# A PEER feed-forward block: 32 tokens taken out of the dense up products and computed from gathered expert rows

## The reference

```python
# T = 512 tokens, D = 1024, 8 heads, 128 x 128 = 16384 experts, top 16 per head
q = (ht @ peer_wq).reshape(T, 8, 2, 128)
s = einsum('thpd,hpkd->thpk', q, peer_keys)
sv, si = top_k(s, 16)                       # per half of the key
cand = sv[..., 0, :, None] + sv[..., 1, None, :]
top, pos = top_k(cand, 16)                  # 16 experts per token and head
eidx = ...                                  # expert = i * 128 + j
g = softmax(top)
u = peer_u[ib]                              # 128 expert rows per token
a = gelu(einsum('td,thkd->thk', hb, u))
out = einsum('thk,thkd->td', g * a, peer_v[ib])
```

## Time and profile before

| | |
|---|---|
| median of 3 runs | 1610.52 us |
| the profiled execution | 1606.33 us, span 1604.5 us |
| PE, weight loads, DVE, ACT, POOL busy | 99%, 86%, 83%, 40%, 25% of the span |
| granted TensorE clock | 1.00 |
| chain that ended last | PE 94%, DVE 3%, ACT 1% |
| HBM | 260 GB/s over the span, 413 in the fullest slice |

### The profile page before, as it was taken

How to read it: one execution, slowest core, us unless ns; L and a number is a source line. 1 busy time by engine, 2 the same in 40 slices (tenths; PEclk the granted TensorE clock), 3 DMA queues, 4 the chain that set the end, 5 groups by cost and what they waited for, 6 DMA issues and landing times.

```text
span 1604.5 us, 24652 instructions
## 1 busy us (share of the span) xinstructions
PE 1582.9 (99%) x8490; PEld 1382.4 (86%) x8490; DVE 1338.7 (83%) x2533; ACT 634.6 (40%) x978; POOL 406.6 (25%) x343
## 2 busy tenths in 40 slices
PE   8999999999999999999999999999999999999998
PEld 4777678887889999999998888888888888888887
DVE  6899787774899999999678888888888888888876
ACT  5433834235334445554333333333333333333332
POOL 0000001102435200001244334433343333433420
PEclk9999999999999999999999999999999999999999
DMA  9431245753324467868999999999999999999981
GB/s 339 144 106 40 99 165 185 254 185 120 109 82 151 156 208 251 279 227 259 387 413 387 352 345 332 333 360 358 343 331 328 357 356 349 329 326 359 355 312 69
DMA packets 168012, 418.79 MB, mean 261 GB/s; under 512 B 12673, under 2 KB 78337, under 8 KB 167810
## 3 DMA queue, kind: packets, MB, share of 16 engines
q1 hardware_dynamic: 115472, 247.92, 42.4%
q0 software_dynamic: 42960, 156.79, 27.3%
q10 hardware_dynamic: 9506, 13.12, 2.2%
HBM read 375.83 MB, written 41.95 MB: 260 GB/s over the span
## 4 chain that ended last, share of the span: by engine, by line
PE 94%; DVE 3%; ACT 1%; issue 1%; DMA 0%; DVEq 0%; ACTq 0%
PE bank L1575 18%; PE bank L1577 17%; PE bank L1576 17%; PE bank L1921 11%; PE bank L1922 11%; PE bank L1920 11%; PE bank L1899 3%; PE bank L1831 1%; DVE sb_scr L1086 1%; PE bank L1748 1%; PE bank L1607 1%; PE bank L1738 1%; PE bank L1609 1%; PE bank L1608 1%; DVE sb_scr L987 1%
## 5 line engine op out<-in xcount | busy, mean ns | idle before, releaser
L625 ACT ACTIVATE sb_w_hi<-sb_stage 128x1024 fp32r<-128x1024 f32 x324 | 343.2, 1061 | 541.8 <-PE bank L1922 323.7
L973 DVE TENSOR_TENSOR sb_w_lo<-sb_stage,sb_w_hi 128x1024 fp32r<-128x1024 f32 x294 | 359.4, 1224 | 169.8 <-ACT sb_w_hi L625 168.6
L1575 PE MATMUL bank<-sb_act_hi,sb_w_hi 128*128 128x384 f32 (+1 forms) x1408 | 498.1, 354 | 2.9 <-DVE sb_w_lo L973 2.2
L1577 PE MATMUL bank<-sb_act_hi,sb_w_lo 128*128 128x384 f32 (+1 forms) x1408 | 492.7, 350 | 0.0
L1576 PE MATMUL bank<-sb_act_lo,sb_w_hi 128*128 128x384 f32 (+1 forms) x1408 | 492.2, 350 | 0.0
L1922 PE MATMUL bank<-sb_w_hi,sb_mix_lo 128*128 128x512 f32 x768 | 300.1, 391 | 0.0
L1921 PE MATMUL bank<-sb_w_lo,sb_mix_hi 128*128 128x512 f32 x768 | 299.9, 391 | 0.0
L1920 PE MATMUL bank<-sb_w_hi,sb_mix_hi 128*128 128x512 f32 x768 | 298.8, 389 | 0.0
L1575 PEld LDWEIGHTS bank<-sb_act_hi,sb_w_hi 128*128 128x128 f32 x1408 | 264.4, 188 | 23.3 <-issue 4.4
L1576 PEld LDWEIGHTS bank<-sb_act_lo,sb_w_hi 128*128 128x128 f32 x1408 | 264.5, 188 | 17.3 <-issue 0.5
L1577 PEld LDWEIGHTS bank<-sb_act_hi,sb_w_lo 128*128 128x128 f32 x1408 | 264.2, 188 | 15.2
(11 more groups left out here) (244 smaller groups left out, 1814.6 us busy)
## 6 DMA issues: line engine op xcount, KB each, us to landing
sb_stage<-u_dram SPq DMA_DIRECT2D x128, 512.0 KB, 5.5
sb_stage<-v_dram SPq DMA_DIRECT2D x128, 512.0 KB, 6.0
sb_stage<-w_front_dram SPq DMA_DIRECT2D x68, 512.0 KB, 4.4
g_scratch<-sb_scr SPq DMA_DIRECT2D x12, 2048.0 KB, 8.8
sb_scr<-g_scratch SPq DMA_DIRECT2D x32, 768.0 KB, 8.0
sb_scr<-w_ada_dram POOLq DMA_DIRECT2D x32, 512.0 KB, 4.6
a_scratch<-sb_scr ACTq DMA_DIRECT2D x64, 192.0 KB, 4.0
sb_scr<-a_scratch SPq DMA_DIRECT2D x16, 768.0 KB, 11.7
```

Source lines behind the costliest of these rows:

```text
L625: nc.scalar.activation(w_hi[:, slot, :], stage[:, slot, :], ACT.Copy).then_inc(w_round, 1)
L973: nc.vector.tensor_tensor(w_lo[:, slot, :], stage[:, slot, :], w_hi[:, slot, :].bitcast(F32), ALU.subtract).then_inc(w_split, 1)
L1575: nc.tensor.matmul(out, w_hi[:, slot, w], rhs_hi[:, dc, :], start=(i == 0), stop=False)
L1577: last = nc.tensor.matmul(out, w_lo[:, slot, w], rhs_hi[:, dc, :], start=False, stop=(i == len(dcs) - 1))
```

## The change

The first 32 tokens of tile 0 (`NS`) leave the dense up products. These run over 352 columns (`NU`), and gelu too; the first 32 columns of `ga` are 1.0 all the time. The gates of these tokens are not made by one-hot products: part 0 of `g_scratch` is filled with zeros early, and for each pick the value weight x gelu(dot) is added into its place by an indirect DMA with addition. As the activation there is 1.0, gate times activation is then what it was.

The dots come from gathered rows. The 32 tokens have 128 picks each. They are laid out as 4 groups of 32 partitions, each group with the same 32 tokens and 32 of the picks, so 32 gathers of 128 rows do (`SPICKS`). For that PE copies the tokens' activations four times into rows (`sh2_ok`), DVE copies them from PSUM to `s_h`, and POOL copies the lists of expert numbers, places and weights to the four groups. DVE makes a dot per gather, two in most units from 1 to 18 of the gate stage, ACT two gelus, DVE two weight products, POOL 32 scatter-adds. The batches of the gate stage are 44 instead of 48: turn 0 has one in each unit. The diff below, cut to its core, shows the constants and tables first, then the parts of POOL, ACT, DVE and PE.

```diff
+NS = 32
+NU = ND - NS
+GROUPS = P // NS
+SPICKS = PICKS // GROUPS
+S_ROWS = 6
+S_HALF = SPICKS // 2
+S_FIRST = (1, 10)
+S_UNITS = 9
...
-def share(n, b):
-
-    return range(n * b // G_UNITS, n * (b + 1) // G_UNITS)
+def batches(it, b):
+
+    skip = S_BATCHES if it == 0 else 0
+    n = TURN_BATCHES - skip
+    return range(skip + n * b // G_UNITS, skip + n * (b + 1) // G_UNITS)
...
+def sparse_dots(u):
+
+    half = int(u >= S_FIRST[1])
+    k = u - S_FIRST[half]
+    return [S_HALF * half + d for d in range(S_HALF) if 0 <= k == d * S_UNITS // S_HALF]
...
             pool.wait_ge(m_ok, DC)
             pool.dma_start(keys[:, :, :], keys_d).then_inc(keys_in, 16)
+            nc.gpsimd.memset(zeros, 0.0).then_inc(gz_ok, 1)
+            pool.wait_ge(gz_ok, 1)
+            for k in range(4):
+                pool.dma_start(g_d[8 * k:8 * k + 8, :, 0:1, :].rearrange("a p n m -> p a (n m)"),
+                               zeros.rearrange("p (o m) -> p o m", o=1).to_broadcast([P, 8, P])).then_inc(gz_in, 16)
...
             pool.wait_ge(x2_out, 16)
...
+            def sparse_gather(d):
+                k = s_pick(d)
+                if d >= S_ROWS:
+                    pool.wait_ge(s_used, d - S_ROWS + 1)
+                pool.indirect_dma_start(s_row[d % S_ROWS], None, u_rows_d,
+                                        bass.IndirectOffsetOnAxis(ap=s_list.bitcast(U32)[:, 0, k:k + 1], axis=0)
+                                        ).then_inc(sg_in[d % S_ROWS], 16)
+
+            def sparse_add(d):
+
+                h, r = divmod(d, SPICKS // PH)
+                k = s_pick(d)
+                if r == 0 and h:
+                    pool.wait_ge(s_out, 16 * (SPICKS // PH) * h)
+                pool.indirect_dma_start(g_flat, bass.IndirectOffsetOnAxis(ap=s_list.bitcast(U32)[:, 1, k:k + 1], axis=0),
+                                        s_w[:, d:d + 1], None, compute_op=ALU.add).then_inc(s_out, 16)
+
+            pool.wait_ge(st_ok, 1)
+            for g in range(GROUPS):
+                pool.dma_start(s_list[g * NS:(g + 1) * NS, :, :],
+                               m_list[0:NS, :, g * SPICKS:(g + 1) * SPICKS]).then_inc(sl_in, 16)
+            pool.wait_ge(sl_in, 16 * GROUPS)
+            pool.wait_ge(gz_in, 64)
+            for d in range(S_HALF + S_ROWS):
+                sparse_gather(d)
+            pool.wait_ge(sw_ok, 1)
+            for d in range(S_HALF):
+                sparse_add(d)
+                if S_HALF + S_ROWS + d < SPICKS:
+                    sparse_gather(S_HALF + S_ROWS + d)
+            pool.wait_ge(sw_ok, 2)
+            for d in range(S_HALF, SPICKS):
+                sparse_add(d)
             pool.wait_ge(idx_ok, 1)
...
-                    nc.scalar.activation(ga[:, k % 2, :], UB[k][:, 0:ND], ACT.Gelu).then_inc(ge_ok, 1)
+                    nc.scalar.activation(ga[:, k % 2, NS:ND], UB[k][:, 0:NU], ACT.Gelu).then_inc(ge_ok, 1)
...
+                    for half in range(2):
+                        if it * G_UNITS + b == S_FIRST[half] + S_UNITS:
+                            act.wait_ge(s_used, S_HALF * (half + 1))
+                            d = slice(S_HALF * half, S_HALF * (half + 1))
+                            nc.scalar.activation(s_gelu[:, d], s_dot[:, d], ACT.Gelu).then_inc(sd_ok, 1)
...
+                    if tt == 0:
+                        link(nc.vector.tensor_tensor(rank_eq[:, 0:4 * P], sums[:, 0:4 * P], sums[:, 4 * P:8 * P], ALU.add))
+                        link(nc.vector.tensor_tensor(rank_eq[:, 0:2 * P], rank_eq[:, 0:2 * P], rank_eq[:, 2 * P:4 * P], ALU.add))
+                        link(nc.vector.tensor_tensor(ijw[0][:, part, :], rank_eq[:, 0:P], rank_eq[:, P:2 * P], ALU.add))
...
+            for half in range(2):
+                dve.wait_ge(sh2_ok, DC // 2 * (half + 1))
+                nc.vector.tensor_copy(s_h[:, half * 512:half * 512 + 512], UB[2 + half][:, :]).then_inc(sh2_cp, 1)
             for h in range(PH):
                 topk_pair([(0, h), (1, h)])
...
+            def sparse_dot(d):
+                dve.wait_ge(sg_in[d % S_ROWS], 16 * (d // S_ROWS + 1))
+                nc.vector.tensor_tensor_reduce(s_row[d % S_ROWS], s_row[d % S_ROWS], s_h, 1.0, 0.0, ALU.mult, ALU.add,
+                                               s_dot[:, d:d + 1]).then_inc(s_used, 1)
...
             def g_turn(it, first):
                 weight_parts(it)
                 for b in range(G_UNITS):
                     split_unit(it * G_UNITS + (FRONT + G_FIRST + b + 2), (FRONT + G_FIRST + b + 2) % RING)
-                    for n in share(TURN_BATCHES, b):
+                    for n in batches(it, b):
                         hot_batch(it, n, first)
+                    for d in sparse_dots(it * G_UNITS + b):
+                        sparse_dot(d)
+                    for half in range(2):
+                        if it * G_UNITS + b == S_FIRST[half] + S_UNITS + 1:
+                            sparse_weights(half)
                     if b in PIECE_UNITS:
                         indices(it + 1, PIECE_UNITS.index(b))
...
+                    for g in range(GROUPS):
+                        last = nc.tensor.matmul(UB[2 + m // 4][g * NS:(g + 1) * NS, m % 4 * P:(m % 4 + 1) * P],
+                                                wide[:, m, 0:NS], ident, start=True, stop=True)
+                    last.then_inc(sh2_ok, 1)
...
-                product(UB[b % 4][:, 0:ND], b % RING, range(DC), act_hi[:, :, 0:ND], act_lo[:, :, 0:ND]
+                product(UB[b % 4][:, 0:NU], b % RING, range(DC), act_hi[:, :, NS:ND], act_lo[:, :, NS:ND]
                         ).then_inc(w_used, 1)
```

More of the change, by code:

```diff
@@ L270, in block_program @@
         g3 = at(13696, [P])
+        s_row = [spare[:, k * D:(k + 1) * D] for k in range(S_ROWS)]
+        s_h = spare[:, 6144:6144 + D]
+        m_list = spare[:, 7168:7168 + 3 * PICKS].rearrange("p (c k) -> p c k", c=3)
+        s_list = spare[:, 7552:7552 + 3 * SPICKS].rearrange("p (c k) -> p c k", c=3)
+        s_dot = spare[:, 7648:7648 + SPICKS]
+        s_gelu = spare[:, 7680:7680 + SPICKS]
+        s_w = spare[:, 7712:7712 + SPICKS]
+        zeros = at(4096, [P])
+        place = const[:, 3 * P + 16:3 * P + 17]
         xend = at(0, [DC, T])
@@ L404, in block_program @@
         fin_ok = sem("fin_ok")
+        gz_ok = sem("gz_ok")
+        gz_in = sem("gz_in")
+        one_ok = sem("one_ok")
+        sh2_ok = sem("sh2_ok")
+        sh2_cp = sem("sh2_cp")
+        st_ok = sem("st_ok")
+        sl_in = sem("sl_in")
+        s_out = sem("s_out")
+        sg_in = [sem(f"sg_in{i}") for i in range(S_ROWS)]
+        s_used = sem("s_used")
+        sd_ok = sem("sd_ok")
+        sw_ok = sem("sw_ok")
         def sums_read(n):
@@ L478, in _ @@
                 part, rest = divmod(q - 6 - G_FIRST, G_UNITS * TB // TURN_TOKENS)
-                if q >= G_FIRST + 6 and rest == 2 and part < ND // TB:
+                if q >= G_FIRST + 6 and rest == 2 and 1 <= part < ND // TB:
                     gate_write(part)
@@ L876, in g_turn @@
                         list_copies(it + 1, (G_FIRST + LIST_UNIT + 2) % 4)
[L878 removed]
+                    for half in range(2):
[3 more added lines that the diff above has]
+                            nc.scalar.activation(s_gelu[:, d], s_dot[:, d], ACT.Gelu).then_inc(sd_ok, 1)
+                    for j in [2 * n + k for n in batches(it, b) for k in range(2)]:
                         part, o = divmod(4 * j, TB)
                         s = part % 2
[L881 to L883 removed]
+                        written = (it * TURN_TOKENS // TB + part) // 2 - (s == 0)
+                        if o == 0 and written > 0:
+                            act.wait_ge(gw_out[s], 16 * written)
+                        act.wait_ge(g_ok, group_no(it, j) + 1)
                         nc.scalar.activation(gb[:, s, :, o:o + 4], bank[j % 4][:, :].rearrange("p (t j) -> p j t", t=4),
@@ L1409, in hot_batch @@
                 s = n % 2
-                if not (first and n < 2):
-                    dve.wait_ge(g_ok, it * (TURN_TOKENS // 4) + 2 * (n - 1))
+                if batch_no(it, n) >= 2:
+                    dve.wait_ge(g_ok, 2 * (batch_no(it, n) - 1))
                 numbers = ijb[:, it * TURN_BATCHES + n, :, :].rearrange("p c (a o b) -> p (c a) o b", o=1, b=2)
@@ L1890, in g_turn @@
                         lists(it + 1, it * G_UNITS + G_FIRST + b)
-                    for t in [n * HB + k for n in share(TURN_BATCHES, b) for k in range(HB)]:
+                    for t in [n * HB + k for n in batches(it, b) for k in range(HB)]:
                         j, n = t // 4, t // HB
-                        if t % 4 == 0 and not (first and j < 4):
-                            pe.wait_ge(g_cp, it * (TURN_TOKENS // 4) + (j - 3))
+                        if t % 4 == 0 and group_no(it, j) >= 4:
+                            pe.wait_ge(g_cp, group_no(it, j) - 3)
                         if t % HB == 0:
-                            pe.wait_ge(hot_ok, it * TURN_BATCHES + n + 1)
```

(2 more changed lines are left out.)

59 lines of the change are left out of this document (47 added, 12 removed).

## The result

The changed kernel takes 1616.86 us, the median of 6 runs (1614.16 to 1618.70); the kernel before took 1609.38 us on the same chip (6 runs, 1606.53 to 1610.99). The ratio is 1.0046, with a 95% interval of 1.0034 to 1.0058: slower by 5.5 to 9.3 us. Forecast were 1621.2 us, 1608 to 1640, and slower with a chance of 0.81. The profiled execution took 1616.89 us with a span of 1614.9, which is 10.4 more than the span of before (forecast: 10.7).

A forecast was written before the change was run, and what follows sets the result against it. PE alone was taken to bound the kernel outside the gate stage, DVE inside it. Terms summed to +33.7 us at slab 56, less 23.0: +10.7, 1617.0 profiled, 1621.2 us as a median; range 1608 to 1640 (8 in 10).

The forecast's parts named there:

- Term B: Slabs 0 to 20: faster slabs' gain lost in PE's wait for lists; extra DVE list work, +3.7 us.
- Term C: Gate stage on DVE: dots added, one-hot batches removed, some waits for ACT recovered; +26.2 us.
- Terms D and E: Gate stage: DVE waits for gathered rows, first rows +1 us, rows fetched between scatter-adds +1.5 us.
- Term F: Leaving the gate stage: slab 56 starts sooner after DVE's last gate product, PE waiting for it; -1.8 us.
- Term A: Front: PE's four extra products per chunk, turning 32 tokens into rows; +3.1 us at 64 ns a record.
- rival 2: Gate stage: POOL's row chain decides, DVE stops before dots; about +15 us beyond the terms, 1636 us; chance 0.17.
- Term G: After gate stage, slabs 56 to 63 and fused loop: PE alone decides, 72 slabs save 0.32 us each, -23.0 us.
- 1, DVE not the pacer: Gate stage: DVE doesn't set it, or swallows much of the 33.7 us; faster if under 23.0 us; chance 0.13.
- 3, 0.10 us a slab: Up products on PE: narrowing saves 0.10 us a slab instead of 0.32; +26.5 us, 1637 us; chance 0.05.
- 4, the clock: Gate stage: PE idle a quarter of it, its clock falls to 1.2 GHz; +72 us, 1693 us; chance 0.03.

The follow-up runs named there:

- cols384: The changed kernel with its up products back over all 384 columns, gelu still reading 352: 1646.34 us, ratio 1.0226 to the kernel before.
- only352: The kernel before with only its up products narrowed to the upper 352 of 384 columns: 1578.04 us, ratio 0.9808.
- thin_dots: The changed kernel with each of its 32 dots over the first 128 of 1024 elements: 1601.69 us, ratio 0.9951 to the kernel before.
- warm: The changed kernel with six extra 352-column products ahead of each slab of the gate stage: 1626.85 us, ratio 1.0118 to the kernel before.
- pool_splits: The kernel before with the `w_lo` subtractions of 13 of the gate stage's units moved from DVE to POOL: 1624.87 us, ratio 1.0104.

## Why the prediction was right

**The bound.** "The stage lasts as long as DVE's instructions" held: 13 us of PE's work in or out left it at 230 us, and 5 us less of DVE's waiting made it 5 us shorter.

**The sum.** +10.7 us was forecast between the profiled executions, and +10.4 came. The mechanism of the large terms was right, but that the total is so close is luck: B came out 4.1 us lower and C 2.0 lower, D and E together 3.8 higher and F 1.4 higher, and these nearly cancel. The medians differ by 7.5 us only, because the profiled execution of before lay 3.1 us under its median of six runs, and that of the changed kernel at its median (1616.89 and 1616.86). The prediction added 4.2 us for such a difference to get its median, which is why 1621.2 is 4.3 us too high.

**Term A**, +3.1: measured +3.28 (14.76 to 18.04), 68 ns a record against the 64 taken.

**Term B**, +3.7: +3.5 at equal width. But the step "these slabs' gain is lost in that wait, no more" missed a second way: the 4.0 us that DVE's top-k gained through POOL's other timing. The sum said +6.8 for the first one-hot tile, the trace has +3.2 (571.00 against 567.82).

**Term C**, +26.2: DVE's busy time rose by 28.0 (190.93 to 218.89), where 39.0 - 9.6 + 0.6 = 30.0 were reckoned. Its other idle time fell from 8.7 to 11.2 - 6.3 = 4.9 us, so 3.8 recovered, as reckoned. Together +24.2.

**Terms D and E**, +2.5: +6.3. The second dot's row was 5.0 us late, where the term for all first rows was 1.0 with an end of 4. The gathers took POOL 937 to 2012 ns, as bounded, but landed after 4.8 to 9.8 us (median 7.9) where 4.6 to 7.1 was taken for the first ones. The first dot was on time at 578.57; the second gather, issued at 574.96, landed 9.8 us later, and the second dot waited for it until 584.79. The expected trouble, the adds between the rows, cost 1.3. What rival 2 made of the doubled gathers is borne out: the 46 gathers of the kernel before and the 9 of the changed one that had no DVE instruction beside them all took 0.93 to 0.94 us of POOL, and the longest of each, 1.98 and 2.01 us, began within 0.1 us of a `w_lo` subtraction on DVE. The scatter-adds on POOL (min/median/max ns; what POOL waited for before them):

```profile
L673 POOL DMA_INDIRECT g_scratch<-sb_spare x32: 1553/2024/2624, 652.6 to 770.8; - x32
...
  DMA g_scratch<-sb_spare: 31.4, 7
```

A scatter-add took 2.0 us to issue where 0.94 + 0.3 was taken, and POOL waited 31.4 us for them, but that was not DVE's time.

**Term F**, -1.8: -0.4. PE was not waiting at the end; it came out of its slab at 801.69, 0.6 us after DVE's tile, and had the products of both last batches still to do, 1.8 us.

**Term G**, -23.0: -22.9, by two errors that cancel, which is luck. A slab saves more than 0.32 us: 0.36 in slabs 56 to 63 (2.88 in all), and 0.39 in a step of the loop, whose length went from 12.39 to 11.99 us (the forecast had 12.36 and 12.04), 24.8 over the loop. And at the loop's entry, from slab 64 to slab 65, the changed kernel loses 4.75 us. PE stands still there, its only wait after the gate stage, and the next products then start 0.43 us apart instead of 0.23:

```profile
841.28 0.74 PE L2076 MATMUL bank<-sb_w_hi,sb_mix_hi 128*128 128x512 f32 x1 [3.32 <-DVE sb_mix_lo L1578]
841.83 0.63 PE L2077 MATMUL bank<-sb_w_lo,sb_mix_hi 128*128 128x512 f32 x1
842.25 0.63 PE L2078 MATMUL bank<-sb_w_hi,sb_mix_lo 128*128 128x512 f32 x1
...
845.02 0.40 PE L2076 MATMUL bank<-sb_w_hi,sb_mix_hi 128*128 128x512 f32 x1
845.25 0.39 PE L2077 MATMUL bank<-sb_w_lo,sb_mix_hi 128*128 128x512 f32 x1
```

The granted clock was 0.53 on average from 841.2 to 844.8. The 18 products of this step took 5.79 us, against 4.17 before: 1.6 us of the 4.75 are the clock.

The chain that leads to the wait, in order of time (start us, us, what):

```profile
812.02 10.81 DMA sb_stage<-u_dram
822.86 1.07 ACT sb_w_hi L726
823.95 1.24 DVE sb_w_lo L1083
825.20 13.85 DMA sb_stage<-v_dram
839.08 0.34 ACT sb_w_hi L726
...
840.58 0.57 DVE sb_mix_lo L1578
841.28 0.74 PE bank L2076
```

Between 800 and 840 the DMA engines were full (share 1.03, 387 GB/s), since the gates' and activations' transfers run there beside the weights. From the gates' end to slab 65 it took 44.52 us before, 44.47 with `cols384`, 44.37 with `only352` and 46.02 after: the 384-column kernels just fill that time with PE's work, without a gap, and the 352-column ones don't go below it. `only352` also waited 3.30 us there, but its products kept their 0.23 us; the 1.65 us between it and the changed kernel are the slower clock. "DMA from 0.89 to 0.91, so neither takes over" was an average over 760 us, and the place where a transfer decides was 40 us long. That the transfers set this floor is read from the chain; no run took them away.

**The rivals.** 1, DVE not the pacer: ruled out (`cols384`). 2, the rows' chain: it was there, but the limit that it sets was some 17 us short of DVE's (`thin_dots`). 3, 0.10 us a slab: ruled out by 158.3 ns. 4, the clock: its mechanism appeared; in the gate stage it cost next to nothing (`warm`), at the loop's entry 1.6 us, nothing like the 72 of the rival. The granted clock over two stretches of the changed kernel's gate stage, and products at the lower level:

```profile
580.00:600.00 20.00, 12.60 (x99) 12.19 (x99) 14.94 (x23) 5.42 (x10) 7.77 (x7) 0.83 0.80 285
...
660.00:680.00 20.00, 13.20 (x88) 12.44 (x87) 18.21 (x26) 5.77 (x10) 15.55 (x9) 0.77 0.77 227
```

```profile
594.81 0.49 PE L1727 MATMUL bank<-sb_act_hi,sb_w_lo 128*128 128x352 f32 x1
...
595.11 0.49 PE L1725 MATMUL bank<-sb_act_hi,sb_w_hi 128*128 128x352 f32 x1
```

0.30 us apart, at 1.2 GHz, after PE had stood still 7.4 us. The prediction's "against" (PE had waited in other stages at clock 1.00) was wrong: in the stage it fell most where PE paused longest, at slab 22 (13.26 us to the next) and slab 34 (12.69 us), and it was 1.00 from 720 to the stage's end, where PE's pauses were short.

## What to carry to other kernels

Where two engines are level in a stage, work put on the one that sets the pace is paid nearly in full, and work taken from the other saves next to nothing (2.2 of 13 us in `only352`, none in the changed kernel); count the saving only for the stages in which the relieved engine decides. Before POOL is called free, look for DVE operations beside it, those with two SBUF inputs above all: in `pool_splits` 11 of 13 subtractions on POOL cost DVE the rest of their time. A saving on PE ends where a transfer becomes late; ask for it in windows of tens of us, not over the loop. A lower granted clock matters where PE sets the pace right after a pause, and not where another engine does.
